# Stick-breaking V products of the sample streams on column strips, weights and values swapped

## The reference

```python
def stick_breaking(q, k, v, q_pos, k_pos):
    z = einsum('bqhd,bkhd->bhqk', q, k) * (SB_HEAD_DIM ** -0.5)
    mask = k_pos[None, :] < q_pos[:, None]
    log_keep = where(mask, -softplus(z), 0.0)
    rev = cumsum(log_keep, axis=3, reverse=True)
    excl = concatenate([rev[..., 1:], zeros_like(rev[..., :1])], axis=-1)
    a = where(mask, exp(log_sigmoid(z) + excl), 0.0)
    return einsum('bhqk,bkhd->bqhd', a, v)
# samples: k and v are 256 cached ones and the 16 new ones of each stream
```

## Time and profile before

| | |
|---|---|
| median of 3 runs | 1836.77 us (1836.74 to 1837.48) |
| span of the profiled execution | 1835.9 us |
| PE busy | 1791.2 us, 98% |
| PEld busy | 1602.2 us, 87% |
| DVE busy | 942.2 us, 51% |
| ACT busy | 687.7 us, 37% |
| stick-breaking stage | from about 60 to 409 us of the span |

### The profile page before, as it was taken

One profiled execution on the slowest core, in us unless ns is written; L12 is line 12 of the kernel. 1 busy time (PEld: TensorE's weight loads), 2 busy tenths in 40 slices (PEclk: granted clock), 3 DMA queues, 4 the chain that ended last, 5 costly groups with the idle time before them and its releaser, 6 DMA issues. The chain is left out here.

```text
span 1835.9 us, 24835 instructions
## 1 busy us (share of the span) xinstructions
PE 1791.2 (98%) x10388; PEld 1602.2 (87%) x10388; DVE 942.2 (51%) x1308; ACT 687.7 (37%) x978; POOL 24.7 (1%) x46
## 2 busy tenths in 40 slices
PE   9999999999999979999999999999999999999998
PEld 8777778889999979889988998989898989899896
DVE  6586777667776797454353633323323233323334
ACT  5677677653433455123451411203020211212122
POOL 1000000000000000000000000000000000000001
PEclk9999999999999999999999999999999999999999
DMA  5312122110111242612431111111011111111102
GB/s 181 99 55 74 47 74 66 55 46 26 48 48 37 71 147 96 232 46 69 115 93 35 39 42 50 43 46 47 24 58 35 47 46 40 30 58 35 46 24 104
DMA packets 147936, 118.02 MB, mean 64 GB/s; under 512 B 4593, under 2 KB 129137, under 8 KB 147826
## 3 DMA queue, kind: packets, MB, share of 16 engines
q1 hardware_dynamic: 147826, 116.44, 20.5%
HBM read 98.40 MB, written 18.02 MB: 63 GB/s over the span
## 5 line engine op out<-in xcount | busy, mean ns | idle before, releaser
L225 ACT ACTIVATE sbuf_w_hi<-sbuf_raw 128x1024 fp32r<-128x1024 f32 x116 | 121.7, 1053 | 382.1 <-PE PS L2128 315.4
L2082 PE MATMUL PS<-sbuf_h_hi,sbuf_w_hi 128*128 128x384 f32 x768 | 256.8, 334 | 0.0
L2084 PE MATMUL PS<-sbuf_h_hi,sbuf_w_lo 128*128 128x384 f32 x768 | 256.6, 334 | 0.0
L2083 PE MATMUL PS<-sbuf_h_lo,sbuf_w_hi 128*128 128x384 f32 x768 | 256.6, 334 | 0.0
L2180 DVE TENSOR_TENSOR sbuf_X<-PS,sbuf_X 128x512 f32<-128x512 f32 x144 | 99.5, 691 | 251.6 <-PE PS L2128 251.4
L2127 PE MATMUL PS<-sbuf_w_hi,sbuf_u_lo 128*128 128x512 f32 x576 | 227.2, 395 | 0.0
L2128 PE MATMUL PS<-sbuf_w_lo,sbuf_u_hi 128*128 128x512 f32 x576 | 227.2, 395 | 0.0
L2126 PE MATMUL PS<-sbuf_w_hi,sbuf_u_hi 128*128 128x512 f32 x576 | 227.2, 394 | 0.0
L566 PE MATMUL PS<-sbuf_h_hi,sbuf_w_hi 128*128 128x384 f32 x600 | 212.7, 355 | 6.4 <-ACT sbuf_g_N L577 3.0
L568 PE MATMUL PS<-sbuf_h_hi,sbuf_w_lo 128*128 128x384 f32 x600 | 202.0, 337 | 0.0
L567 PE MATMUL PS<-sbuf_h_lo,sbuf_w_hi 128*128 128x384 f32 x600 | 202.0, 337 | 0.0
(11 more groups left out here) (263 smaller groups left out, 2938.7 us busy)
## 6 DMA issues: line engine op xcount, KB each, us to landing
sbuf_raw<-w_ffn SPq DMA_DIRECT2D x64, 512.0 KB, 4.0
sbuf_raw<-w_in SPq DMA_DIRECT2D x28, 512.0 KB, 4.9
sbuf_X<-x_prompt SPq DMA_DIRECT2D x16, 512.0 KB, 6.2
sbuf_s_cK<-cache_sb_k SPq DMA_DIRECT2D x8, 512.0 KB, 4.6
sbuf_s_cV<-cache_sb_v SPq DMA_DIRECT2D x4, 1024.0 KB, 5.6
sbuf_raw<-w_out SPq DMA_DIRECT2D x8, 512.0 KB, 4.1
out_yp<-sbuf_X SPq DMA_DIRECT2D x8, 512.0 KB, 2.6
sbuf_r_lo<-mixT SPq DMA_DIRECT2D x7, 576.0 KB, 8.9
```

Of the source, the lines that this page charges most:

```text
L225: act.activation(w_hi[s][:], raw[s % 2][:], ACT.Copy).then_inc(cut_hi[s % 2], 1)
L2082: pe.matmul(out, hi, h_hi[:, kb, tok], start=kb == 0, stop=False)
L2083: pe.matmul(out, hi, h_lo[:, kb, tok], start=False, stop=False)
L2084: last = pe.matmul(out, lo, h_hi[:, kb, tok], start=False, stop=kb == KB - 1)
```

## The change

The samples' V products are written the other way round. The turned attention weights of one stream (128 keys x 32 columns) stand, the values (128 keys x 128 features) move, and the result, 32 rows for each stream, lands on the strip of partitions 32s of bank 6, in columns 256 to 511. Four streams take the four strips in turn. The new values are a third round of the same four strips. The result has frames on the partitions, so ScalarE copies it to a new tile s_tok (`tokens`), and TensorE turns it back in two transposes (`sample_turn`), issued at the end of unit 9, into columns 0 to 255, from where VectorE copies as before, now after a wait for sb_tn.

HALVES moves one half group from unit 10 to unit 9 in pairs 0 to 2. It stands there between av(8) and t(9). The rest of the diff merges semaphores: one order counter for VectorE in three stages, one semaphore for two loads or for two steps with doubled counts.

```diff
-        HALVES = (1, 2, 2, 1, 1, 1, 1, 2, 2, 0, 2, 2, 1)
+        HALVES = (1, 2, 2, 1, 1, 1, 1, 2, 2, 1, 1, 2, 1)
...
                     for g in range(2):
-                        o_ = PS[:, 6, g * P:(g + 1) * P]
-                        w = s_aT[:, g, :]
-                        pe.matmul(o_, vt[:, SMP, :], w[:, 2 * P:3 * P], start=True, stop=False,
-                                  skip_group_check=True)
-                        for s in range(4):
-                            for kt in range(2):
-                                last = pe.matmul(o_[:, s * 32:(s + 1) * 32], s_cV[:, 8 * g + 2 * s + kt, :],
-                                                 w[:, kt * P + s * 32:kt * P + (s + 1) * 32],
-                                                 start=False, stop=kt == 1, skip_group_check=True)
+                        for kt in range(3):
+                            for s in range(4):
+                                v_ = s_cV[:, 8 * g + 2 * s + kt, :] if kt < 2 else vt[:, SMP, :]
+                                last = pe.matmul(PS[32 * s:32 * s + 32, 6, (2 + g) * P:(3 + g) * P],
+                                                 s_aT[:, g, kt * P + s * 32:kt * P + (s + 1) * 32], v_,
+                                                 start=kt == 0, stop=kt == 2)
                 last.then_inc(sb_av, 1)
+
+            def sample_turn(p):
+
+                pe.wait_ge(sb_tk, p + 1)
+                for g in range(2):
+                    last = pe.transpose(PS[:, 6, g * P:(g + 1) * P], s_tok[:, g * P:(g + 1) * P], ident)
+                last.then_inc(sb_tn, 1)
...
                 if len(fills(u)) < 2:
                     transposes(u)
+                if v == US + 1:
+                    sample_turn(p)
...
+            def tokens(u):
+
+                act.wait_ge(sb_av, u + 1)
+                if u // UP:
+                    act.wait_ge(sb_tn, u // UP)
+                act.activation(s_tok[:], PS[:, 6, 2 * P:4 * P], ACT.Copy).then_inc(sb_tk, 1)
...
                 copy_extra(u)
+                if u % UP == US + 1:
+                    tokens(u - 1)
                 if not behind and not inside:
                     copy_next(u)
...
                     dve.tensor_copy(s_o[:, i * P:(i + 1) * P], PS[:, 6, 0:P]).then_inc(sb_o, 1)
                     return
+                dve.wait_ge(sb_tn, p + 1)
```

## The result

The changed kernel takes 1829.03 us, median of 6 runs (1827.67 to 1831.35), against 1837.12 for the kernel before (6 runs). The ratio is 0.995, with a 95% interval of 0.9936 to 0.9964: faster by 0.5%, some 9 us by the ratio and 8 by the medians. The forecast was 1826.7, in a range of 1823 to 1833. A second set of 5 runs gave 0.9961 (0.9947 to 0.9974), so 7 us.

A forecast was written before the change was run, and what follows sets the result against it. TensorE, busy 98% of the span, was taken as the bound, with VectorE's exponents as second chain. Pair gains 1.69 + 2.71 + 3.45 + 2.22 = 10.1 us; 1836.8 - 10.1 = 1826.7 us, range 1823 to 1833.

The forecast's parts named there:

- av(8): V products of unit 8, the samples' unit, in each stick-breaking head pair; 3.93 us before, 1.45 us forecast after.
- t(9): TensorE's transposes of unit 9 in a head pair; 0.90 us forecast, with 0.26 us for the two transposes back behind.
- X: Time of the samples' new V products on TensorE; 1.45 us forecast, bounds 1.35 and 3.2 us.
- A: Rival at the samples' V products: strips share no time, 0.11 us each, products 5.3 us, kernel 1842; chance 0.03.
- B: Rival at the samples' V products: no help beyond two strips, 0.068 us each, products 3.2 us, kernel 1833.7; chance 0.10.
- VectorE's chain: Copy of the transposes back, then unit 11's exponent (5.00 us), holding unit 13's scores until 11.87 us in pair 0.
- z(13): Scores of unit 13, counted from unit 11's scores: forecast at 11.87 us in pair 0, after waiting 0.9 us for VectorE.
- Just covered: V products of units 9 and 10 need copies at 6.81 and 12.25 us, and stand at 6.91 and 12.29: no wait.
- The copy to s_tok: ScalarE's copy before the transposes back: free behind the fill; without that cover 0.4 us and a semaphore's way.
- The clock: TensorE's clock behind the samples' products: the fill splits that stretch, clock taken to stay at 2.4 GHz in pair 1.
- D: Rival in the stage behind, led by VectorE some 15 us: gain given back; 1832 if half lost; chance 0.05.
- C: Rival: clock falls anyway in pairs 1 or 2, or the shift moves a fall elsewhere; 1828.5 to 1831; chance 0.22.

The follow-up runs named there:

- two of the edits here: Against the changed kernel: one more half group moved from unit 11 to unit 10, 1830.73 us; transposes back issued before unit 9's own transposes, 1831.93 us in one execution.

## Why the prediction was right, and where it was off

**X.** 1.45 us was forecast from L699's beat of four, and 1.45 was measured. Rivals A and B are out: 1.45 / 48 is 0.030 us for each load and matmul. So are, for this shape, the 81 ns of the Trainium skill (TensorE: Matmul & The Clock Gate, Back-to-back issue gap). A's price of 0.11 us is what one strip takes from one instruction to the next, in either order of the strips; what it has wrong is that the strips share no time.

**VectorE's chain.** z(13) was to wait 0.9 us for exponent(11) and to come at 11.87; it waited 0.78 and came at 11.53. The larger mis-sized term is t(9) with the transposes back: 0.90 + 0.26 were put down, and 125.60 - 124.64 = 0.96 measured. The 0.90 held the step from transposes to scores, which now stands behind the two added ones; it was not one of t(9) itself. The other 0.13 us are on VectorE: its copy was to start 0.31 us behind z(12), and started 0.18 behind it (125.78 - 125.60). Pair 0 gained 2.03 at z(13) where 1.69 was forecast, pair 1 3.06 for 2.71, pair 2 3.47 for 3.45, pair 3 2.34 for 2.22. "Just covered" was right for av(9) and av(10): in pairs 0 and 1 neither waits; in pair 2 av(10) does, 0.17 us. The fill-only kernel shows that av(10) loses the cover of the moved fill; the prediction saw it, as a near miss.

**The copy to s_tok** costs nothing behind the fill, as forecast. The price without that cover, 0.4 us and a semaphore's way, rested on "ScalarE was free there", and it was not: the 1.61 us of idle time in the earlier trace rows begin at 125.90 - 1.61 = 124.29, and the products end at 122.45. The swap alone shows the price, 1.32 us.

**The clock.** That it would stay up behind av(8) was right, the reason given was not. With the fill "splitting that stretch" it was to stay at 2.4 GHz; but the fill alone left it falling, 5 times in the 8 pairs of two traces. These are all falls behind the products, by pair, in all traces:

| products | fill moved | traces | pairs with a fall |
|---|---|---|---|
| before | no | 2 | 1, 2; then 0, 2 |
| before | yes | 2 | 0, 3; then 0, 1, 2 |
| new | no | 2 | 2; then 2 |
| new | yes | 7 | none of 28 |

So the old products draw the clock down (9 of 16 pairs), with or without a fill behind. With the new ones a fall came only in pair 2 without the fill, where TensorE waits 1.32 and 2.30 us. So in pair 1 the swap was enough to keep the clock up, and in pair 2 it took the swap and the fill together. What in the old products does it, their 32 moving columns or the time that weight loads take, was not taken apart. Some 2.3 us of the 10.7 are falls that are gone: 1.0 in pair 1 (21.31 against 20.30 in pair 0), and 1.3 in pair 2, estimated from pair 0's way from z(12) to z(14): 7.45 + 20.30 - 5.89 = 21.86, against 23.20.

**The sum.** 10.1 us were forecast for what the stage gained as 10.7. The medians moved by 6 to 8, the ratios say 7 to 9. The step that was off is the one that let the next stage shift as a whole (D, and the second half of C). From the first transposes of that stage to the first product of the output projection the two traces of the kernel before take 321.5 and 321.7 us, the changed kernel 322.1 and 324.9, with no edit to its work in between. That the two spans differ by just the 10.1 of the forecast is luck: it is 10.7 less 0.6. The stretch of 640 to 730 us holds the falls of the clock in both; whole stretch, before, then after in its second trace:

```profile
640.00:730.00 90.00, 80.17 (x614) 74.30 (x613) 77.85 (x113) 51.45 (x66) 2.51 (x2) 0.96 0.32 110
```

```profile
640.00:730.00 90.00, 84.09 (x574) 78.65 (x575) 73.41 (x112) 50.48 (x64) 2.51 (x2) 0.87 0.31 102
```

The mean granted clock is 0.96 against 0.87. Over all 13 traces that stage took 319.4 to 326.5 us, and its length goes with its mean clock: 319.4 to 321.5 us at 0.99, 321.0 to 321.7 at 0.98, 322.1 to 324.1 at 0.97, 324.9 to 326.5 at 0.96. So a part of the gain, 0.6 us in one trace and 3.4 in the other, was given back there to the clock. The earlier start isn't needed for it: the kernel with the fill alone starts that stage at 409.5, as the kernel before does (409.0), and took 326.5 us. Whether it is chance which kernel gets the long ones, these few traces don't settle. The forecast had counted this with a chance of 0.22 and 0.05 and left it out of the likeliest case; by the medians some 2 us of it belonged there.

**The moved fill** was costed at nothing but the 0.30 us of L577's wait, which is gone. Alone it costs 0.23 us a pair at the full clock; beside the swap it is worth 0.66, because it hides the copy to s_tok. The two parts of the change are worth more together (2.05 us in pair 0) than alone (1.39 and -0.23).

## What to carry to other kernels

Where few columns moved over full weights (32 over 128, 0.117 us each), swapping the sides and spreading the result over column strips took 3.93 us down to 1.45, and four strips in turn took 42% less time than strip by strip. A step that is added as copy and turn back costs its 0.3 us only if other work lies between its parts: here the half group did, to within 0.05 us. When an added wait can't be removed at a gain, look for a second queue that ends at the same time: two of the edits here brought nothing or a loss alone, and the third, an order of two copies on ScalarE, made one of them worth 0.86 us a pair. Then follow the gain to the end of the stage: in pair 2 the next wait took it back.

## What was not expected of the hardware

The clock can fall while the profile shows TensorE without idle time: in the fill-only kernel it was busy 6.00 of 6 us both before the fall and in it. And the falls wander between executions of the same program: pairs 1 and 2, then 0 and 2. Column strips overlap in either order of issue: a strip takes a new instruction every 0.11 us at 128 columns, and the next strip's start beside it at once when the strips take turns, or 0.25 us later when each strip's six stand in a row.
